# Order of the context-state products in a Mamba-2 layer: weighed by group, two chunks in place, three pairs of split weights

## The reference, cut to what matters

```python
def branch(h, rows_, cols_, need_z):
    ...
    xbc = silu(depthwise_conv_grid(proj[..., :SSM_CONV_DIM], conv_w, conv_b, rows_, cols_))
    dt = softplus(proj[..., SSM_CONV_DIM:] + dt_bias)
    xs, bm, cm = ...   # 2048 columns of x, 512 of B, 512 of C
...
xdt = (xs * dt[..., None]).reshape(b, nc, Q, G, R, P)         # chunks of Q = 128 tokens
decay_to_end = exp(a_cum[:, :, -1:] - a_cum)
chunk_states = einsum('bclgn,bclgrp->bcgrpn', bc, xdt * decay_to_end[..., None])
...
yc, s_f, s_b = scans(xc, bmc, cmc, dtc, zeros, zeros, ctx_out)   # context: states only
yl, _, _ = scans(xl, bml, cml, dtl, s_f, s_b, True)              # latent starts from them
```

## Time and profile before

| | |
|---|---|
| median of 3 runs | 1847.78 us (1847.56 to 1849.45) |
| the profiled execution: own time | 1853.19 us |
| its span | 1851.4 us |
| PE busy | 1652.4 us (89%) |
| DVE busy | 1437.0 us (78%) |
| ACT busy | 596.5 us (32%) |
| POOL busy | 535.4 us (29%) |
| granted TensorE clock, mean | 0.976 of full |

### The profile page before, as it was taken

How to read it: one execution, slowest core, us unless ns; L and a number is a source line. 1 busy time by engine, 2 the same in 40 slices (tenths; PEclk the granted TensorE clock), 3 DMA queues, 4 the chain that set the end, 5 groups by cost and what they waited for, 6 DMA issues and landing times.

```text
span 1851.4 us, 18455 instructions
## 1 busy us (share of the span) xinstructions
PE 1652.4 (89%) x5526; PEld 915.8 (49%) x5526; DVE 1437.0 (78%) x3475; ACT 596.5 (32%) x1486; POOL 535.4 (29%) x542
## 2 busy tenths in 40 slices
PE   7998999999989987989899999899899877778776
PEld 4886688545544433334343778555444423333332
DVE  3988895877677778988887789887777788777755
ACT  4654754232222223333322221122223233222222
POOL 0432000034333333333343000133334334333342
PEclk9999999999999999999999999999999999998999
DMA  9532249899999999999999666699999999999996
GB/s 363 194 114 86 114 163 366 334 368 427 427 424 427 427 425 427 393 426 427 416 420 426 251 263 226 251 427 426 427 426 424 426 427 427 420 415 415 423 428 260
DMA packets 98006, 664.35 MB, mean 359 GB/s; under 512 B 11596, under 2 KB 13613, under 8 KB 19954
## 3 DMA queue, kind: packets, MB, share of 16 engines
q0 software_dynamic: 74304, 536.90, 69.4%
q1 hardware_dynamic: 23602, 126.27, 17.8%
HBM read 662.01 MB, written 1.11 MB: 358 GB/s over the span
## 4 chain that ended last, share of the span: by engine, by line
PE 52%; DMA 29%; DVE 13%; issue 2%; ACT 2%; SPq 0%; PEld 0%; PEldq 0%; POOL 0%; DVEq 0%; POOLq 0%; ACTq 0%
DMA expert_rows<-in_p_uv,chosen_experts 24%; PE bank L1233 19%; PE bank L890 6%; DVE dot_products L2605 6%; PE bank L1367 4%; DMA expert_rows_spare<-in_p_uv,chosen_experts 4%; PE bank L1189 3%; PE bank L1014 3%; PE bank L1091 3%; PE bank L1449 1%; PE bank L1029 1%; PE bank L1002 1%; DMA BC_T<-in_ada_front 1%; ACT weight_diagonal L1785 1%; PE bank L1399 1%
## 5 line engine op out<-in xcount | busy, mean ns | idle before, releaser
L1233 PE MATMUL bank<-expert_rows,weight_diagonal 128*128 128x512 f32 x1816 | 854.7, 612 | 144.1 <-ACT weight_diagonal L1785 143.7
L2605 DVE SCALAR_TENSOR_TENSOR dot_products<-expert_rows,bank 128x1024 f32<-128x1024 f32 x454 | 554.2, 1221 | 213.3 <-DMA expert_rows<-in_p_uv,chosen_experts 201.7
L1233 PEld LDWEIGHTS bank<-expert_rows,weight_diagonal 128*128 128x128 f32 x1816 | 338.1, 194 | 597.0 <-issue 347.8
L1500 POOL DMA_INDIRECT expert_rows<-in_p_uv,chosen_experts x450 | 423.7, 941 | 696.5 <-PE bank L1233 654.1
L1785 ACT ACTIVATE weight_diagonal<-constants,expert_weights 128x128 f32<-128x128 f32 x512 | 178.0, 394 | 242.9 <-DVE expert_weights L2533 241.4
L1777 ACT ACTIVATE expert_gelu<-expert_dots 128x2 f32<-128x2 f32 x260 | 52.8, 203 | 602.8 <-DVE dot_products L2605 602.5
L1500 POOL DMA_INDIRECT expert_rows_spare<-in_p_uv,chosen_experts x58 | 55.2, 952 | 479.5 <-DVE chosen_experts L2518 386.1
L1233 PE MATMUL bank<-expert_rows_spare,weight_diagonal 128*128 128x512 f32 x232 | 114.5, 617 | 20.3 <-ACT weight_diagonal L1785 20.3
L2605 DVE SCALAR_TENSOR_TENSOR dot_products<-expert_rows_spare,bank 128x1024 f32<-128x1024 f32 x58 | 70.8, 1221 | 22.5 <-DMA expert_rows_spare<-in_p_uv,chosen_experts 20.9
L1233 PEld LDWEIGHTS bank<-expert_rows_spare,weight_diagonal 128*128 128x128 f32 x232 | 43.4, 195 | 75.1 <-issue 43.0
L1510 POOL TENSOR_TENSOR weights_lo<-weight_block,weights_hi 128x1024 fp32r<-128x1024 f32 x20 | 48.4, 2424 | 108.8 <-ACT weights_hi L1546 108.8
(11 more groups left out here) (348 smaller groups left out, 2080.0 us busy)
## 6 DMA issues: line engine op xcount, KB each, us to landing
weight_block<-in_m_in_blocks SPq DMA_DIRECT2D x20, 1024.0 KB, 6.7
weight_block<-in_ada_rows SPq DMA_DIRECT2D x18, 1024.0 KB, 6.6
hyena_weight_block<-in_h_in_blocks SPq DMA_DIRECT2D x12, 1024.0 KB, 7.1
hyena_weight_block<-in_ada_rows SPq DMA_DIRECT2D x12, 1024.0 KB, 6.9
weight_block<-in_wq_blocks SPq DMA_DIRECT2D x11, 1024.0 KB, 7.1
expert_rows<-in_p_uv,chosen_experts POOLq DMA_INDIRECT x450, 13.9
x_residual<-in_ada_rows SPq DMA_DIRECT2D x14, 512.0 KB, 3.5
out_weights<-in_m_out_blocks SPq DMA_DIRECT2D x6, 1024.0 KB, 8.2
```

The source lines that it names most:

```text
L1233: last = mm(ps[b][:, :], dg[n % DIAG][:, :], uv[slot][:, D + h * 512:D + (h + 1) * 512], start=(r == 0 and k == 0), stop=end)
L1500: pool.indirect_dma_start(uv[slot][:, :], None, A[f"p_uv{l}"], bass.IndirectOffsetOnAxis(ap=chosen[:, s_, k:k + 1], axis=0)).then_inc(uv_l ...
L2605: stt(prod[:, :], uv[slot][:, 0:D], 1.0, rows_t, ALU.mult, ALU.mult, accum_out=dots[:, s_, k + j:k + j + 1]).then_inc(sem("dots_done"), 1)
```

## The change

Five edits, all in the first layer's convolution and state stage:

1. **Weighing by group.** Chunks 0, 1, 3 and 4 of the six (both context chunks, in both directions) are weighed by group, four pieces of 128x512 at each of the four places where one piece was weighed. The chunks 3 and 4 are weighed in place, over `x_tokens`; chunk 1 goes to a buffer of its own, where the fourth pair of split weights lay. The two latent chunks (2 and 5) are still weighed whole at the end.
2. **Products by group.** PE multiplies groups 0 to 2 of chunks 0 and 1, then group 3 of both; the same for chunks 3 and 4; then chunks 2 and 5.
3. **Banks.** The last two C tiles go to banks 4 and 5, the forward states to 0 to 3, the backward ones to 6, 7, 4, 5.
4. **Three pairs of split weights** in place of four. The low part of tile 3 is made by POOL in place of DVE, and PE multiplies the step sizes ahead of tile 3.
5. **Moved work.** The last six dot products stand at tiles 11, 12, 12, 13, 14, 15 (before: 13 to 18). In ACT's turn 23 the SiLU of tile 21 stands ahead of the centre tap. The copies of the backward context states stand ahead of those of the forward latent ones. The load of gate rows into `ln_gain_bias` waits for the first use alone.

```diff
+STATE_CHUNKS = (0, 1, 2, 1, 0, 3)
-CONV_DOTS = tuple((1, m, q) for m, q in enumerate((1, 1, 2, 3, 4, 5, 6, 7, 13, 14, 15, 16, 17, 18)))
+CONV_DOTS = tuple((1, m, q) for m, q in enumerate((1, 1, 2, 3, 4, 5, 6, 7, 11, 12, 12, 13, 14, 15)))
-SPLITS = 4
+SPLITS = 3
-LO_BY_VECTOR = FRONT_TILES
+LO_BY_VECTOR = SPLITS
...
-    weighed = [lnb..., xw[0][:, :], xw[1][:, :]]
+    weighed = [lnb..., xw_later_chunk[:, :], xw[0][:, :], xtok[:, 1, :], xtok[:, 0, :], xw[1][:, :]]
...
+    for q in range(XBC_CT - 2, XBC_CT):
+        plan.use(("xbc", q), q - XBC_CT + 6)
+    for n in range(2):
+        for d in range(2):
+            for g in range(GROUPS):
+                plan.use((("S1", "S2")[n], d, g), 4 + (g + 2) % 4 if d else g)
...
-        sp.wait_ge(sem("x_weighted_first_used"), 2)
+        sp.wait_ge(sem("x_weighted_first_used"), 1)
...
-        for k in range(KD):
-            front_tiles((3,), k)
...
         step_rows()
+        for k in range(KD):
+            front_tiles((3,), k)
...
+        for first in (0, 3):
+            for groups in (range(GROUPS - 1), range(GROUPS - 1, GROUPS)):
+                for j in (first, first + 1):
+                    for g in groups:
+                        if j == 0:
+                            pe.wait_ge(sem("x_weighted"), 4 * (g + 1))
+                        state_products(j, g, j == first, j > first)
+        for n, j in enumerate((2, 5)):
+            pe.wait_ge(sem("x_weighted"), 4 * GROUPS + n + 1)
+            for g in range(GROUPS):
+                state_products(j, g, True, True)
...
+            if q == XBC_CT - 1:
+                conv_silu(q - 2)
             if q < XBC_CT:
                 ct = conv_tile(q)
...
-            tt(weighed[0][:, x]..., xtok[:, cols[0][1], x]..., bc(wst[:, 0, ...]), ALU.mult)
+            for j in (0, 4, 1, 3):
+                tt(weighed[j][:, x]..., xtok[:, cols[j][1], x]..., bc(wst[:, j, ...]), ALU.mult)
```

More of the change, by code:

```diff
@@ L207, in build_in @@
     lnb = sb(ctx, "ln_gain_bias", [P, 2, D])
-    split_pairs.append(weight_pair(3))
+    with ExitStack() as s:
+        xw_later_chunk = sb(s, "x_weighted_second_chunk", [P, INNER])
     gate = [sb(ctx, f"gate{j}", [P, D]) for j in range(2)]
@@ L267, in build_in @@
     dtw = lnb[:, :, :].rearrange("p a b -> p (a b)")[:, 0:1536].rearrange("p (n c) -> p n c", n=6)
-    weighed = [lnb[:, :, :].rearrange("p a b -> p (a b)"), xw[0][:, :], xw[1][:, :]]
+    weighed = [lnb[:, :, :].rearrange("p a b -> p (a b)"), xw_later_chunk[:, :], xw[0][:, :], xtok[:, 1, :], xtok[:, 0, :], xw[1][:, :]]
     EM = [EM0, [btok[:, 2 * d:2 * d + 2, :].rearrange("p a b -> p (a b)").rearrange("p (h b) -> p h b", h=HPG) for d in range(2)]]
@@ L449, in build_in @@
     plan.use("dt", 7)
-    for q in range(XBC_CT):
+    for q in range(XBC_CT - 2):
         plan.use(("xbc", q), q if q < FRONT_TILES + 2 else (q - FRONT_TILES - 2) % 4)
@@ L985, in _, with state_products @@
         conv_transposes(XBC_CT - 3)
[L987 to L1007, removed]
+        def state_products(j, g, start, stop):
+            d = j // 3
+            key = ("S2" if j % 3 == 2 else "S1", d, g)
+            b = begin(key) if start else plan(key)[0]
+            last = mm(ps[b][:, :], btok[:, STATE_CHUNKS[j], g * P:(g + 1) * P], weighed[j][:, g * GW:(g + 1) * GW], start=start, stop=stop)
+            if stop:
+                last.then_inc(full[b], 1)
+            elif (j, g) == (0, GROUPS - 1):
+                last.then_inc(sem("x_weighted_first_used"), 1)
+        for first in (0, 3):
[9 more added lines that the diff above has]
+                state_products(j, g, True, True)
         def z_products(j, t, k0, k1):
@@ L1560, in _ @@
             if k in FRONT_BLOCKS:
-                for n in range(2):
-                    weights_hi(2 * FRONT_BLOCKS.index(k) + n)
+                for q in range(2 * FRONT_BLOCKS.index(k), min(2 * FRONT_BLOCKS.index(k) + 2, SPLITS)):
+                    weights_hi(q)
         act.wait_ge(sem("dt_weights_in"), 16)
@@ L1578, in quad_rows, with conv_silu @@
                 f(quad[:, n, :], one_or_pair, ACT.Copy, scale=cst[:, C_IOTA, I_QUAD + n:I_QUAD + n + 1])
+        def conv_silu(r):
+            wait_read(act, ("xbc", r))
+            ct = conv_tile(r)
+            if ct >= INNER // P:
+                last = f(bcT[:, ct - INNER // P, :], cacc[r % 3][:, T:2 * T], ACT.Silu)
+            if r in CONV_WITH_CTX:
+                n = CONV_WITH_CTX.index(r)
+                if n >= 2:
+                    wait_full(act, ("xT", n - 2))
+                last = f(xc[n % 2], cacc[r % 3], ACT.Silu)
+            last.then_inc(sem("conv_silu"), 1)
         for q in range(XBC_CT + 2):
@@ L1621, in _ @@
                 copy_out(("xT", n), dst, lambda b: b[:, :].rearrange("p (t c) -> p t c", t=4))
[L1622 to L1633, removed]
+            if q >= 2 and q != XBC_CT - 1:
+                conv_silu(q - 2)
         def sum_rows_split():
@@ L2038, in _ @@
             if k in FRONT_BLOCKS:
-                for n in range(2):
-                    weights_lo(2 * FRONT_BLOCKS.index(k) + n)
+                for q in range(2 * FRONT_BLOCKS.index(k), min(2 * FRONT_BLOCKS.index(k) + 2, SPLITS)):
+                    weights_lo(q)
         dve.wait_ge(sem("dt_weights_hi"), 1)
```

34 lines of the change are left out of this document (9 added, 25 removed).

## The result

| | before | after |
|---|---|---|
| median of 20 runs each | 1849.51 us | 1852.55 us |
| ratio after / before | | 1.0014, 95% interval 1.0008 to 1.0020 |
| profiled execution, span | 1851.4 us | 1850.9 us |
| mean granted clock | 0.976 | 0.977 |

By the ratio the change costs 2.6 us (3.0 us by the two medians) where a gain of 2.9 was forecast. The 20 runs of the kernel before have a median 1.7 us above that of the first three. The two profiled executions lie 0.5 us apart the other way; each is one of 20, and we come back to why. The stage is read from the timelines here. In what follows "before" and "after" stand for the traces of the two kernels.

What follows compares the result with a forecast made beforehand. PE was taken to hold the chain, except where it idles for DVE's taps and weighing before the state products, then runs at half clock. 4.2 - 1.3 - 0 = 2.9 us gain from 1847.8, say 1845 us; range 1841 to 1850.

Steps and rivals of the forecast that it cites:

- The front: Start of the convolution: SP's longer wait makes dot-product rows late, DVE some 5 us late at tile 4; PE loses 0.
- Rival C: Start of the convolution: late dot-product rows make PE wait 4.6 us or more, giving 1849.5 us; chance 0.12.
- When PE can start: End of the convolution: DVE's lateness sets the products' start, at 177.8 us; they end at 198.4, 4.2 us earlier.
- point (2): Expected trace sign: PE idle before the transposes of tile 19, near 169 us, and of tile 21, near 175 to 177.
- point (3): Expected trace sign: the 24 products follow one another without a pause, over 21 to 23 us, from near 178 us.
- The block of a weighing by POOL: Before tile 20: POOL's subtraction stops DVE's weighing, whose four pieces start at 164.2 us; price between 0 and 2.42 us.
- rival A: Before tile 20: the weighing runs beside POOL and the clock stays; gain 6.1 us, giving 1841.7 us; chance 0.24.
- The clock at the products: Start of the state products: half clock after PE's idle time costs 1.3 us, bounds 0 and 3.3.
- point (4): Expected trace sign: granted clock below 1 for less than 4 us around 178 to 182 us.
- Rival B: Start of the state products: clock low for 6.6 us as before, 3.3 us lost; gain 0.9 us, 1846.9 us; chance 0.20.
- The end as a sum: End of convolution and state products: 4.2 us from the earlier end less 1.3 us for the clock, a 2.9 us gain.
- The moved `step_rows` leaves PE the same work, at nothing: Front of the convolution: moving PE's step-size products ahead of tile 3 costs or gains nothing.

Runs made afterwards that it cites:

- run 2: Kernel before, with SP issuing the block of tiles 6 and 7 only after POOL's first low part: 1.0034 of the kernel before.
- run 3: Changed kernel with DVE's copy of the step sizes at the start of turn 3 instead of turn 4: 0.9978 of the kernel before.
- run 4: Changed kernel with POOL's low parts of tiles 21 and 23 waiting until DVE has weighed groups 1 and 2: 0.9995 of the kernel before.
- run 5: Changed kernel, block of tiles 6 and 7 issued behind the first dot products' rows, POOL's low parts of tiles 21 and 23 behind the weighings: 0.9967 of kernel before.
- run 1: Changed kernel with SP issuing the block of tiles 6 and 7 behind the rows of dot products 0 and 1: 0.9976 of the kernel before.
- run 8: Changed kernel, block of tiles 6 and 7 behind the rows, last six dot products back at tiles 13 to 18: 0.9984 of the kernel before.
- run 10: Kernel before with only the three pairs of split weights, block of tiles 6 and 7 behind the rows: 1.0011 of the kernel before.
- run 9: Kernel before with only the three pairs of split weights (low part of tile 3 by POOL, step sizes ahead of tile 3): 1.0034 of the kernel before.
- run 6: Changed kernel, rows ahead of the block of tiles 6 and 7, POOL behind the weighings, step-size copy ahead of dot product 3: 0.9961 of the kernel before.
- run 7: As run 6, but group 2's chunks 4 and 3 weighed with the last group and ACT copying tile 17 before `weights_hi`: 0.9962 of the kernel before.

## Why the prediction was wrong, point by point

- **The failed step** is "The front": "PE sees it only through the SiLU of tile 3 ... Bounds 0 to 1.3 us; I take 0." The lateness itself came out as worked out: rows near 56 (dot product 0 began at 54.61), the third near 63.8 (63.62), DVE "some 5 us late at tile 4" (5.3). What I missed is a second way from DVE to PE. I looked at what PE waits for by data, SiLUs, and not at which bank it needs: `step_copy` stands behind dot product 3 and holds bank 7 for the transposes of tile 1. The plan of banks said so (`"dt"` and `"xT"` 1, both 7). Runs 2 and 3 show it: the wait alone makes the loss, the copy alone takes it away. The term that I took at 0 is +7.3 us in the trace, 4.7 of pause and 2.6 of half clock behind it (6.2 to 7.5 us over the four traces with the pause).
- **Rival C** had the place, SP's wait, and 4.6 us of pause, but by another path (SiLU and step sizes on ACT) and with a chance of 0.12; it had no term for the clock. That its 4.6 us met the measured 4.66 us is luck.
- **When PE can start** was right: the products were to start 17.9 us behind the transposes of tile 17 (159.88 and 177.8), and did (163.48 and 181.41), behind pauses before the transposes of tiles 19 and 21, as in point (2). They followed without a pause, point (3), and the dots and weighings of turns 16 to 18 cost PE nothing more.
- **The block of a weighing by POOL**, which rival A denied: right, twice, and removed by run 4.
- **The clock at the products** (loss 1.3 us): low for under 4 us, as in point (4); it cost 1.7 us where 1.3 was taken (4.28 us from the first of the six records to the next group, against 2.57 in run 5). Rival B, with over 6 us, is out.
- **The end as a sum**: forecast 2.9, in the trace 2.3 (of 43.0 us from the transposes of tile 17 to the first exponential); 0.4 of the difference is the clock.
- **"The moved `step_rows` leaves PE the same work, at nothing"**: the front of three pairs is shorter, a gain I did not cost. At full clock the transposes of tile 0 come at 62.0 to 62.7 in the traces with three pairs and at 63.42 in run 2 with four, about 1.1 us; before's own 64.27 holds the half-clock stretch at 28 us more, as does run 5's 64.24.
- **Sum**: forecast -2.9; by the traces, without the stretches that come and go, +7.3 - 2.3 - 1.1 = +3.9, and the runs say +2.6 by the ratio, +3.0 by the medians. With the lowest price of the front among the four traces, 6.2 us, the sum is +2.8. So the difference lies within what the clock does from trace to trace, and is not settled further.

## What to carry to other kernels

When a wait grows on a queue, follow the late work to every instruction behind it on the waiting engine, and ask of each not only what data it makes but which buffer or bank it frees. Before a wait that is allowed to last, issue what is needed sooner; here it was one statement moved by five. A pause on PE is priced with the half clock that may come behind it: pauses of 4.5 to 5 us cost 6.2 to 7.5 us here, those of about 1.5 us at the same place (runs 1, 5, 8 and 10) cost 1.6 to 1.7 us, little more than themselves.

## What the runs showed of the hardware

- A subtraction on POOL and a multiplication of two SBUF tensors on DVE do not overlap where the subtraction begins first: 2.45 to 2.47 us for a piece of 0.68 while POOL's 2.40 to 2.42 lasts. The other way round POOL is the one that waits: in the trace of after a dot product on DVE starts at 117.61, and the subtraction that starts at 118.12 takes 2.98 us. It is the behaviour that the Trainium skill states (page "SBUF — State Buffer", section "Who interferes with whom"), and the trace of before had shown it only for dot products.
- The granted clock fell to its lower level behind the pauses of PE of 4.5 to 5 us (changed kernel, runs 2, 4 and 9) and of 2.83 us (changed kernel, runs 1, 3 and 8); behind pauses of 2.55 us it fell in run 4 and not in runs 5 and 6; behind those of 1.44 to 1.55 us at tile 1 it stayed (runs 1, 5, 8 and 10). At 112 us it fell in some traces though PE had not paused since 84 us. A gain of 1 us can be taken back by one such stretch, as in run 7.
